# Depthwise convolution taps moved from diagonal matmuls on TensorE to scaled shifts on GpSimd, in an eight-core hybrid block

## Chip, cores and metric

One Trainium2 chip, all 8 cores. The batch has 4 sequences of 4,096 tokens; each core takes one half of one sequence (2,048 tokens), and for the state that the second half starts from it also reads the first half. No core talks to another. The metric is the device time of the slowest core in microseconds, the median over runs.

## What is computed

The block runs a gated linear recurrence (four heads of 128) beside a short gated convolution, merges the two with sigmoid gates, and ends with a SwiGLU feed-forward. The part that matters here is the convolution branch, 512 channels wide, with three causal taps for each channel:

```python
def short_conv_mixer(c_gate, b_gate, xb, conv_w):
    u = c_gate * xb                                          # inner gate C
    rhs = conv_w.astype(u.dtype)[:, None, :]                 # (K, 1, CONV_WIDTH) depthwise
    y = lax.conv_general_dilated(u, rhs, window_strides=(1,), padding=[(CONV_K - 1, 0)],
                                 dimension_numbers=('NWC', 'WIO', 'NWC'),
                                 feature_group_count=CONV_WIDTH)
    return b_gate * y                                        # outer gate B
```

`c_gate`, `xb` and `b_gate` are three slices of the input projection `h @ w_in`, where `h` is the normalised input. So for each channel c and token t, y(t) = w0 u(t-2) + w1 u(t-1) + w2 u(t), and the branch gives b(t) y(t).

## The kernel before

A core's 2,048 tokens are four blocks of T = 512. Activations lie transposed in SBUF, channels in the partitions: `hT0` to `hT3` hold the normalised input of the four blocks as 8 pieces of 128 channels by 512 tokens. Weights come as slabs of 1 MB (in memory) into a ring of 8 buffers, `ring0` to `ring7`, by DMAs that GpSimd issues (line 630); 0 holds the forget gate's slab, 1 the value slab, 2, 3 and 4 those of c, xb and b_gate, and 5, 6 and 7 first serve as buffers for arriving rows of x and later take the slabs of q, g and ga0.

`mm_fm` (line 737 before, 732 after) is the work horse: 8 matmuls of 128x512 into one PSUM bank. `conv_gen(b)` makes block b of the convolution. Its first loop runs over m = 0 to 3 (128 channels each): a c group of 8 matmuls, which ScalarE copies out of PSUM, then an xb group of 8, which VectorE multiplies by that copy into `u`, bf16, 514 columns wide so that two columns of the block before stand ahead. `u` is one buffer with one owner record: whoever reads any part of it waits for all four m, and the next block's first write waits for all of this block's readers. Its second loop, over m again, makes the outer gate. Before, that is 8 matmuls for b_gate and a ScalarE copy of them, then 3 matmuls with diagonal weights `diagw` on `u` shifted by 0, 1 and 2 columns (line 970), and a VectorE product of the two.

The engines' instruction order isn't the order of the program text. Generators are merged into one list of operations, and `Prog.schedule` then plays a list scheduler over it: each operation carries an assumed duration `dur`, each engine picks what it could start first, ties go by the place in the list, among the 48 nearest candidates. What comes out is a fixed order on each engine with semaphore waits. On the chip each engine then works through its own order strictly, so an instruction that waits holds up all behind it.

Around the four convolution blocks lie: norm and transpose work for the coming block (`norm_gen`, transposes at line 764), the recurrence's pass over the earlier half (`pf_gen`, `pv_gen`, `pt_gen`: lines 737, 746, 893, 910), and for block 3 the recurrence proper (`dense_gen` and `core_gen`; lines 1082, 1101, 1121 and 1123 are its small 128x128 matmuls, 1149 the sum over a head with `ones_f`).

Of the kernel before, what the change touches and what calls it, by code (L numbers as in the profile page):

```python
# [7 lines left out]
F32 = mybir.dt.float32  # L8
BF16 = mybir.dt.bfloat16
# [388 lines left out]
def build_nc():  # L398
# [11 lines left out]
    with ExitStack() as st:  # L410
        def sb(name, shape, dt):
            return st.enter_context(nc.sbuf_tensor(name, shape, dt))
# [6 lines left out]
        diagw = sb("diagw", [128, 12, 128], BF16)  # L419
# [277 lines left out]
        def late_consts():  # L697
            P.op("dve", lambda E: E.tensor_copy(out=cmask[:], in_=mskf), reads=[b_mskf], writes=[b_cmask])
            P.op("dve", lambda E: E.memset(ones_f[:], 1.0), writes=[b_ones])
            P.op("dve", lambda E: E.memset(smask[:], 1.0), writes=[b_smask])  # L700
            P.op("dve", lambda E: E.memset(smask[:].rearrange("p (c j) -> p c j", j=CH)[:, :, 0:1], 0.0),
                 reads=[b_smask], writes=[b_smask])
            for i in range(2):
                P.op("dve", lambda E, i=i: E.memset(AT[i][:], 0.0), writes=[b_AT[i]])
            for k in range(12):
                P.op("dve", lambda E, k=k: E.tensor_scalar(out=diagw[:, k, :], in0=ident[:], scalar1=cst[:, CW + k:CW + k + 1],
                                                           scalar2=0.0, op0=ALU.mult, op1=ALU.add),
                     reads=[b_ident, b_cst], writes=[b_diagw])
# [724 lines left out]
```

How the kernel before makes its waits and increments, by code:

```python
        def run(E, e):  # L300
            known = {}
            own = "P_" + e
            for i in self.order[e]:
                o = ops[i]
                need = {}
                for d in list(o.deps) + o.extra:
                    k, v = val[d]
                    if need.get(k, 0) < v:
                        need[k] = v
                for k, v in need.items():
                    if k == own and e == "pe":
                        continue
                    if known.get(k, 0) >= v:
                        continue
                    known[k] = v
                    E.wait_ge(self.sems[k], v)
                if o.chan is not None:
                    o.fn(E).then_inc(self.sems[o.chan], 16)
                else:
                    o.fn(E).then_inc(self.sems[own], 1)
            if e == "sp":
                for b in finals:
                    k, v = val[b.w]
                    if known.get(k, 0) < v:
                        known[k] = v
                        E.wait_ge(self.sems[k], v)
```

## Time and profile before

| | before |
|---|---|
| median of 3 runs | 1044.02 us (1042.1 to 1044.39) |
| profiled execution, its own time | 1040.56 us |
| span of its slowest core (core 5) | 1038.9 us (others 1034.0 to 1038.7) |
| TensorE matmul busy | 1005.8 us, 97% of the span |
| VectorE busy | 463.7 us, 45% |
| ScalarE busy | 414.9 us, 40% |
| GpSimd busy | 23.2 us, 2% |

The profiled execution's own time is 1.7 us more than the span. Busy times of one engine are sums over its instructions without overlap. Matmuls overlap in the pipeline, so a lone matmul's duration (379 ns for 128x512) is longer than the pitch at which a row of them proceeds; what a group costs is read from the rows of the chain, in which each piece follows the one before.

### The profile page before, as it was taken

To read this page: it belongs to the slowest core of one execution; us is meant where nothing else is said; L and a number is where in the kernel's file an instruction comes from. 1 tells how busy PE (TensorE), PEld (TensorE's weight loads), DVE (VectorE), ACT (ScalarE), POOL (GpSimd) and SP (SyncE) were. 2 spreads that over 40 slices of the span, in tenths; PEclk is the share of its full clock that TensorE was granted. 3 is DMA by queue.
4 is the path that set the end of the run, shared out by engine and by line. 5 is a ranking of instruction groups with operands and counts; after the bars stand their busy time and mean duration, and the time that the engine had idled before them with its cause. 6 is when DMAs were issued, how large, how long until landed. Compare 5 with 4: busy or idle time off the path is not lost.

```text
span 1038.9 us, 15069 instructions; the slowest of 8 cores (1034.0 to 1038.9 us)
## 1 busy us (share of the span) xinstructions
PE 1005.8 (97%) x5414; PEld 490.1 (47%) x5414; DVE 463.7 (45%) x651; ACT 414.9 (40%) x706; POOL 23.2 (2%) x49
## 2 busy tenths in 40 slices
PE   4799999999999999999999899999999999999997
PEld 4555545454545454444444444444444444444444
DVE  5777665576667576436564331212121121232223
ACT  3895743768677675233343321111111111111112
POOL 2000000000000000000000000000000000000000
PEclk9999999999999999999999999999999999999999
DMA  9993334033000262542337544020302216222211
GB/s 196 227 225 103 84 62 82 1 60 64 1 1 2 38 99 67 88 115 87 118 122 156 153 97 81 1 41 1 65 17 37 45 17 202 102 106 102 81 61 62
DMA packets 20233, 84.88 MB, mean 82 GB/s; under 512 B 2368, under 2 KB 2368, under 8 KB 16960
## 3 DMA queue, kind: packets, MB, share of 16 engines
q0 software_dynamic: 5904, 33.03, 19.3%
q1 hardware_dynamic: 14112, 50.62, 14.5%
q8 instruction: 45, 0.74, 0.3%
q14 instruction: 28, 0.23, 0.1%
q10 hardware_dynamic: 144, 0.26, 0.1%
HBM read 100.16 MB, written 16.78 MB: 113 GB/s over the span
## 4 chain that ended last, share of the span: by engine, by line
PE 93%; DMA 3%; ACT 2%; issue 1%; DVE 1%; SPq 0%; ACTq 0%; POOL 0%; DVEq 0%; POOLq 0%
PE pf L737 62%; PE pf L1284 15%; PE pf L746 9%; PE pf L764 2%; DMA ring<-x_prev 1%; PE pf L1149 1%; ACT arena L715 1%; DMA ring<-wall 1%; PE pf L970 1%; PE pf L795 1%; DVE arena L864 0%; PE pf L1121 0%; PE pf L830 0%; PE pf L1082 0%; PE pf L1101 0%
## 5 line engine op out<-in xcount | busy, mean ns | idle before, releaser
L737 PE MATMUL pf<-hT,ring 128*128 128x512 bf16 x2688 | 599.2, 379 | 2.3 <-ACT arena L715 1.9
L737 PEld LDWEIGHTS pf<-hT,ring 128*128 128x128 bf16 x2688 | 261.6, 98 | 314.4 <-issue 5.2
L1284 PE MATMUL pf<-ring,arena 128*128 128x512 bf16 (+1 forms) x726 | 152.2, 373 | 0.0
L715 ACT ACTIVATE arena<-pf 128x512 f32<-128x512 f32 (+3 forms) x164 | 99.0, 643 | 97.5 <-PE pf L737 86.1
L715 ACT ACTIVATE rtmp<-pf 128x512 f32<-128x512 f32 (+1 forms) x89 | 52.9, 595 | 186.8 <-PE pf L737 186.8
L1284 PEld LDWEIGHTS pf<-ring,arena 128*128 128x128 bf16 x726 | 71.0, 98 | 81.2
L719 DVE TENSOR_TENSOR arena<-rtmp,pf 128x512 bf16<-128x512 f32 (+1 forms) x69 | 46.9, 679 | 133.0 <-PE pf L737 128.2
L746 PE MATMUL pf<-ring,arena 128*128 128x512 bf16 x384 | 91.1, 384 | 3.7 <-DMA ring<-wall 3.4
L737 PE MATMUL pf<-arena,ring 128*128 128x512 bf16 x320 | 79.8, 379 | 0.9 <-ACT arena L715 0.9
L715 ACT ACTIVATE rtmp<-hT 128x1024 bf16<-128x1024 f32 (+2 forms) x18 | 17.3, 963 | 123.3 <-DVE hT L719 123.3
L719 DVE TENSOR_TENSOR arena<-arena 128x512 bf16<-128x512 f32 (+2 forms) x62 | 55.6, 897 | 23.1 <-ACT arena L715 20.8
L746 PEld LDWEIGHTS pf<-ring,arena 128*128 128x128 bf16 x384 | 37.5, 99 | 47.7 <-issue 6.1
L719 DVE TENSOR_TENSOR hT<-pf,hT 128x512 f32<-128x512 f32 (+1 forms) x33 | 22.3, 675 | 75.2 <-PE pf L1284 75.2
L715 ACT ACT_TABLE_LOAD x36 | 46.2, 1283 | 5.9 <-PE pf L1149 4.1
L727 DVE SCALAR_TENSOR_TENSOR arena<-arena,pf 128x512 f32<-128x512 f32 x44 | 30.1, 686 | 39.8 <-PE pf L737 33.6
L737 PEld LDWEIGHTS pf<-arena,ring 128*128 128x128 bf16 x320 | 30.1, 98 | 33.0 <-issue 1.5
L715 ACT ACTIVATE rtmp<-arena 128x1024 bf16<-128x1024 f32 (+1 forms) x24 | 25.3, 1053 | 45.9 <-DVE arena L727 45.9
L719 DVE TENSOR_TENSOR arena<-Wt,pf 128x512 bf16<-128x512 f32 x22 | 15.1, 688 | 60.0 <-PE pf L737 58.2
L719 DVE TENSOR_TENSOR hT<-pf,cst_sb 128x1024 bf16<-128x1024 bf16 x32 | 38.1, 1217 | 7.5 <-PE pf L764 7.5
L719 DVE TENSOR_TENSOR arena<-U,pf 128x512 bf16<-128x512 f32 x22 | 15.1, 687 | 58.1 <-PE pf L737 58.1
L630 POOL DMA_DIRECT2D ring<-wall x41 | 22.0, 538 | 830.0 <-PE pf L737 554.4
L715 ACT ACTIVATE arena<-ring 128x1024 bf16<-128x1024 f32 x32 | 33.8, 1056 | 15.2 <-PE pf L764 9.2
(96 smaller groups left out, 664.2 us busy)
## 6 DMA issues: line engine op xcount, KB each, us to landing
ring<-wall POOLq DMA_DIRECT2D x25, 1024.0 KB, 11.1
ring<-x_prev SPq DMA_DIRECT2D x16, 512.0 KB, 8.8
ring<-x_main SPq DMA_DIRECT2D x16, 512.0 KB, 4.7
arena<-x_main SPq DMA_DIRECT2D x16, 512.0 KB, 4.5
x1spill<-arena SPq DMA_DIRECT2D x16, 512.0 KB, 2.9
hT<-x1spill SPq DMA_DIRECT2D x16, 512.0 KB, 3.2
out<-hT SPq DMA_DIRECT2D x15, 512.0 KB, 2.6
ring<-wall POOLq DMA_DIRECT2D x6, 512.0 KB, 6.4
```

Source lines behind the costliest of these rows:

```text
L630: P.dma("pool", lambda E, s=s, idx=idx, a=a, z=z: E.dma_start(out=ring[s][:, a:z], in_=w_d[idx][:, a:z]), reads=need(gates[q]) if q < len( ...
L715: P.op("act", lambda E: E.activation(out=rs(out), in_=rs(in_), func=func, **kw), reads=reads, writes=writes, dur=dur, aset=ASET[func] if f ...
L719: P.op("dve", lambda E: E.tensor_tensor(out=rs(out), in0=rs(a), in1=rs(b), op=op), reads=reads, writes=writes, dur=0.17 + width(out, a, b) ...
L727: P.op("dve", lambda E: E.scalar_tensor_tensor(out=rs(out), in0=rs(a), scalar=s, in1=rs(b), op0=op0, op1=op1), reads=reads, writes=writes, ...
L737: last = E.matmul(pb(bk)[:, 0:ncol], lhsT=sl[:, o_:o_ + 128], rhs=rhs[:, c, :], start=(c == 0), stop=(c == kc - 1))
L746: last = E.matmul(pb(bk), lhsT=lhs(c), rhs=rhs_list[c], start=(c == 0), stop=(c == n - 1))
L764: last = E.transpose(out=tbv.res()[:, c * 128:(c + 1) * 128], in_=xs[:, c * 128:(c + 1) * 128], identity=ident[:])
L795: last = E.matmul(pb(bk)[:, c0:c0 + nc_], lhsT=sl[:, o_:o_ + 128], rhs=rhs[:, c, c0:c0 + nc_], start=(c == 0), stop=(c == 7), skip_group_c ...
L970: last = E.matmul(pb(by), lhsT=diagw[:, k * 4 + m, :], rhs=u[:, m, k:k + T], start=(k == 0), stop=(k == 2))
L1149: P.op("pe", lambda E, bk=bk, c=c: E.matmul(pb(bk), lhsT=ones_f[:], rhs=sqs[c][0], start=True, stop=True), reads=[b_ones, sqs[c][1]], writ ...
L1284: last = E.matmul(pb(bk)[:, 0:w], lhsT=act_v(c)[:, n * 128:(n + 1) * 128], rhs=rl[c], start=(c == 0), stop=(c == 21))
```

## The change

The diagonal weights and their 48 matmuls go, with the 12 VectorE instructions that made them, and so do the 16 ScalarE copies of b_gate. In their place GpSimd computes, for each block and each m, three scaled shifts of `u` (`pts`, one input, 128x512, bf16 in and float32 out) and two sums of these (`ptt`, two float32 inputs), into a scratch tile `a`. Then come the 8 matmuls for b_gate. They list `a` among what they read, so TensorE waits there for the whole GpSimd chain of this m, although the matmuls themselves don't touch it. VectorE then multiplies `a` by the PSUM bank.

Blocks 0 to 2 have two pairs of scratch tiles (`rtmp`, four tiles), block 3 has one pair (in `arena`). The c copies go to a new buffer `cvs` of two tiles.

```diff
-        def conv_gen(b, singles):
+        def pts(out, a, sc, reads, writes):
+            P.op("pool", lambda E: E.tensor_scalar(out=out, in0=a, scalar1=sc, scalar2=0.0, op0=ALU.mult, op1=ALU.add),
+                 reads=reads, writes=writes, dur=0.7)
+
+        def ptt(out, a, b, reads, writes):
+            P.op("pool", lambda E: E.tensor_tensor(out=out, in0=a, in1=b, op=ALU.add), reads=reads, writes=writes, dur=1.3)
...
+        def conv_gen(b, singles, tmps):
...
             for m in range(4):
+                (a, b_a), (q, b_q) = tmps[0], tmps[1]
+                if len(tmps) > 2:
+                    (a, b_a), (q, b_q) = tmps[2 * (m % 2)], tmps[2 * (m % 2) + 1]
+                pts(a, u[:, m, 0:T], cst[:, CW + m:CW + m + 1], [b_u, b_cst], [b_a])
+                pts(q, u[:, m, 1:T + 1], cst[:, CW + 4 + m:CW + 5 + m], [b_u, b_cst], [b_q])
+                ptt(a, a, q, [b_a, b_q], [b_a])
+                pts(q, u[:, m, 2:T + 2], cst[:, CW + 8 + m:CW + 9 + m], [b_u, b_cst], [b_q])
+                ptt(a, a, q, [b_a, b_q], [b_a])
                 bb = F_()
-                mm_fm(bb, sg, b_sg, m, 8, 0, hT, b_h)
-                i = cyc("p1s", singles)
-                actf(single(i), bank(bb), AF.Copy, [bb.buf], [b_T[i]])
+                mm_fm(bb, sg, b_sg, m, 8, 0, hT, list(b_h) + [b_a])
+                tt(yb_[b][0][:, m, :], a, bank(bb), ALU.mult, [b_a, bb.buf], [yb_[b][1]])
                 yield 8 * MMC
-                by = F_()
-
-                def fn(E, m=m, by=by):
-                    last = None
-                    for k in range(3):
-                        last = E.matmul(pb(by), lhsT=diagw[:, k * 4 + m, :], rhs=u[:, m, k:k + T], start=(k == 0), stop=(k == 2))
-                    return last
-                P.op("pe", fn, reads=[b_diagw, b_u], writes=[by.buf], dur=3 * MMC)
-                tt(yb_[b][0][:, m, :], single(i), bank(by), ALU.mult, [b_T[i], by.buf], [yb_[b][1]])
-                yield 3 * MMC
```

**TensorE, block 0.** The first fence is TensorE's order before, from the last xb group (`ring3`) of block 0 through its four b_gate groups (`ring4`):

```order
L737 MATMUL pf<-hT0,ring3 128x512 x8
L764 MATMUL pf<-ident,arena 128x128 x8
L737 MATMUL pf<-hT0,ring4 128x512 x8
L970 MATMUL pf<-arena,diagw 128x512 x3
L737 MATMUL pf<-hT0,ring4 128x512 x8
L764 MATMUL pf<-ident,arena 128x128 x8
L970 MATMUL pf<-arena,diagw 128x512 x3
L737 MATMUL pf<-hT0,ring4 128x512 x8
L970 MATMUL pf<-arena,diagw 128x512 x3
L737 MATMUL pf<-hT0,ring4 128x512 x8
L970 MATMUL pf<-arena,diagw 128x512 x3
```

The second is the same place after the change, from that same xb group to b_gate group 1:

```order
L732 MATMUL pf<-hT0,ring3 128x512 x8
L759 MATMUL pf<-ident,arena 128x128 x24
L888 MATMUL pf<-ident,arena 128x128 x8
L741 MATMUL pf<-ring1,arena 128x512 x8
L759 MATMUL pf<-ident,arena 128x128 x8
L741 MATMUL pf<-ring1,arena 128x512 x8
L905 MATMUL pf<-arena 128x128 x16
L759 MATMUL pf<-ident,arena 128x128 x8
L732 MATMUL pf<-hT0,ring4 128x512 x8
L741 MATMUL pf<-ring1,arena 128x512 x8
L732 MATMUL pf<-hT0,ring4 128x512 x8
```

It goes on with 8 transposes and 8 value matmuls, group 2, a c and an xb group of block 1, and group 3. The `ring4` groups, which used to follow the xb group at once, are now pulled apart, and other work stands in the gaps. What follows the last of them is held up with it.

**VectorE, block 2.** The next fence is VectorE's order after the change, from the last product into `u` of block 2 (`arena<-cvs,pf`) to the outer-gate products of m = 0 (first `arena<-rtmp,pf` behind the scan), 1, 2 and 3:

```order
L714 TENSOR_TENSOR arena<-cvs,pf 128x512
L714 TENSOR_TENSOR hT3<-pf,cst_sb 128x8x128 x2
L718 TENSOR_SCALAR arena<-arena,sv 128x512 x2
L815 SCALAR_TENSOR_TENSOR arena<-smask,arena 128x1024
L714 TENSOR_TENSOR arena<-rtmp,pf 128x512
L714 TENSOR_TENSOR arena<-arena 128x1024
L714 TENSOR_TENSOR arena<-rtmp,pf 128x512
L718 TENSOR_SCALAR arena<-arena,sv 128x512 x2
L714 TENSOR_TENSOR arena<-arena 128x1024
L958 COPY arena<-arena 128x4x2
L714 TENSOR_TENSOR arena<-rtmp,pf 128x512 x2
```

While GpSimd works on block 2's taps, VectorE has four scalings, a scan (printed as SCALAR_TENSOR_TENSOR with `smask`) and two products of two SBUF tensors of 1,024 columns to do. Counted in the same way, block 0 has six scalings of 1,024 columns (`arena<-ring,stat`) in that stretch, and block 1 four. In block 3 the same stretch holds four scalings of 512 columns, two scans, four products or sums of two SBUF tensors of 1,024 columns and five of 512.

**TensorE, block 3.** The last fence is TensorE's order after the change, from two of the `ones_f` sums to the third b_gate group of block 3; dense work of the recurrence's block 1 (`hT1` with `ring0`, `ring1`, `ring5`, `ring6`) stands between the groups:

```order
L1156 MATMUL pf<-arena,ones_f 128x512 x2
L732 MATMUL pf<-hT1,ring0 128x512 x8
L732 MATMUL pf<-hT3,ring4 128x512 x8
L1156 MATMUL pf<-arena,ones_f 128x512
L732 MATMUL pf<-hT1,ring0 128x512 x24
L732 MATMUL pf<-hT3,ring4 128x512 x8
L741 MATMUL pf<-ring1,hT1 128x512 x32
L732 MATMUL pf<-hT3,ring4 128x512 x8
```

Here the next m's chain can only start when the product of the m before has freed the one scratch tile, so the groups stand further apart; before, all four groups of this block stood ahead of the `ones_f` sums.

## Rows read from the trace of the kernel before

**Rows 1.** The page: busy time and instructions; the span in 40 slices, busy tenths.

```profile
PE 1005.8 (97%) x5414; PEld 490.1 (47%) x5414; DVE 463.7 (45%) x651; ACT 414.9 (40%) x706; POOL 23.2 (2%) x49
PE   4799999999999999999999899999999999999997
```

**Rows 2.** Busy time by stretch: length, busy (instructions), clock, DMA share, GB/s.

```profile
0.00:84.00 84.00, 62.72 (x589) 42.12 (x590) 57.02 (x88) 60.76 (x118) 7.13 (x19) 0.98 0.86 201
84.00:240.00 156.00, 153.50 (x901) 77.10 (x899) 94.90 (x128) 88.12 (x153) 3.69 (x7) 1.00 0.33 71
```

**Rows 3.** The chain that ended last, 100 to 240 us: start, length, what.

```profile
99.97 3.02 PE pf L737 x14
...
105.82 1.73 PE pf L737 x8
...
112.74 0.65 PE pf L970 x3
113.39 0.46 PE pf L764 x8
...
120.29 0.89 PE pf L910 x16
...
220.76 0.67 PE pf L1082 x12
...
235.24 3.43 PE pf L1149 x8
```

**Rows 4.** Instructions by shape: busy, mean ns of one, idle before them.

```profile
L970 PE MATMUL pf<-arena,diagw 128*128 128x512 bf16 x48 | 13.0, 379 | 0.0
L706 DVE TENSOR_SCALAR diagw<-ident,cst_sb 128x128 bf16<-128x128 bf16 x12 | 3.1, 262 | 1.0
L715 ACT ACTIVATE rtmp<-pf 128x512 f32<-128x512 f32 x88 | 52.8, 600 | 186.8 <-PE pf L737 186.8
```

**Rows 5.** GpSimd in order of time, 0.5 to 4 us: start, length.

```profile
0.60 0.10 POOL L399 MEMSET const-uint8-127<- 128x1 uint8 x1
...
3.04 0.22 POOL L678 MEMSET Wt<- 128x128 f32 x1
3.40 0.29 POOL L679 TENSOR_SCALAR_AFFINE_SELECT Wt<-Wt 128x128 f32<-128x128 f32 x1
```

**Rows 6.** VectorE in order of time, 102 to 104 us: start, length, wait ahead.

```profile
103.10 0.69 DVE L719 TENSOR_TENSOR arena<-rtmp,pf 128x512 bf16<-128x512 f32 x1 [2.10 <-PE pf L737]
```

**Rows 7.** GpSimd and VectorE in order of time, 6.2 to 7 us.

```profile
6.42 0.55 POOL L630 DMA_DIRECT2D ring<-wall  x1 [2.73 <-DMA ring<-x_prev]
6.62 0.35 DVE L706 TENSOR_SCALAR diagw<-ident,cst_sb 128x128 bf16<-128x128 bf16 x1
```

**Rows 8.** VectorE instructions by shape, as in rows 4.

```profile
L723 DVE TENSOR_SCALAR arena<-ring,stat 128x1024 bf16<-128x1024 f32 x32 | 23.6, 749 | 10.2 <-ACT stat L715 10.2
L723 DVE TENSOR_SCALAR arena<-arena,sv 128x512 f32<-128x512 f32 x32 | 16.4, 541 | 26.6 <-ACT arena L715 26.6
L820 DVE TENSOR_TENSOR_SCAN arena<-smask,arena 128x1024 f32<-128x1024 bf16 x8 | 18.3, 2286 | 0.6 <-ACT rtmp L715 0.5
L719 DVE TENSOR_TENSOR arena<-arena 128x1024 bf16<-128x1024 f32 x16 | 19.5, 1222 | 5.9 <-ACT arena L715 5.8
L719 DVE TENSOR_TENSOR Wt<-U,Gd 128x512 f32<-128x512 f32 x16 | 11.0, 686 | 0.9 <-DVE U L719 0.9
```

**Rows 9.** GpSimd in order of time, 84 to 260 us.

```profile
139.24 0.53 POOL L630 DMA_DIRECT2D ring<-wall  x1 [78.86 <-DVE arena L723]
...
167.80 0.53 POOL L630 DMA_DIRECT2D ring<-wall  x1 [13.67 <-ACT arena L715]
```

**Rows 10.** The longest of those transfers: microseconds from issue to landing, 100 to 240 us.

```profile
DMA to landing us min/median/max: 7.6/9.7/14.1
```

**Rows 11.** TensorE's waits, 0 to 300 us: microseconds in total, times, longest.

```profile
PE pf L764 <- DVE arena L723: 15.1, 5, 11.1
PE pf L737 <- ACT arena L715: 2.9, 3, 1.9
```

More of the change, by code:

```diff
@@ L418, in build_nc @@
         smask = sb("smask", [128, 2 * T], BF16)
-        diagw = sb("diagw", [128, 12, 128], BF16)
+        cvs = sb("cvs", [128, 2, T], F32)
         U = sb("U", [128, 4, 128], F32)
@@ L473, in bufs @@
             return [Buf(f"{pre}{i}") for i in range(n)]
-        b_cst, b_ident, b_ones, b_cmask, b_smask, b_diagw, b_U, b_W, b_sv, b_e1, b_G, b_e2l, b_zcol, b_hcol = (
-            Buf(n) for n in ["cst", "ident", "ones", "cmask", "smask", "diagw", "U", "W", "sv", "e1", "G", "e2l", "zcol", "hcol"])
+        b_cst, b_ident, b_ones, b_cmask, b_smask, b_U, b_W, b_sv, b_e1, b_G, b_e2l, b_zcol, b_hcol = (
+            Buf(n) for n in ["cst", "ident", "ones", "cmask", "smask", "U", "W", "sv", "e1", "G", "e2l", "zcol", "hcol"])
         b_Sb, b_AT, b_stat = bufs("Sb", 2), bufs("AT", 2), bufs("stat", 8)
@@ L704, in late_consts @@
                 P.op("dve", lambda E, i=i: E.memset(AT[i][:], 0.0), writes=[b_AT[i]])
[L705 to L708, printed above, removed]
         ASET = {AF.Exp: 1, AF.Ln: 1, AF.Silu: 2, AF.Tanh: 2}
@@ L919, in build_nc @@
         P1S = [10, 11, 12, 13]
+        P1T = [(single(i), b_T[i]) for i in P1S]
         def halo_gen():
@@ L940, in halo_gen @@
                ALU.mult, [bx.buf, b_T[i]], [b_u])
-        def conv_gen(b, singles):
+        def pts(out, a, sc, reads, writes):
[3 more added lines that the diff above has]
+            P.op("pool", lambda E: E.tensor_tensor(out=out, in0=a, in1=b, op=ALU.add), reads=reads, writes=writes, dur=1.3)
+        b_cvs = bufs("cvs", 2)
+        CVS = [(cvs[:, i, :], b_cvs[i]) for i in range(2)]
+        cv3 = []
+        for i in range(2):
+            v, bb = area(f"cv3_{i}", O_MG + 2 * 4096 + 2048 * i, 2048, F32)
+            cv3.append((v, bb))
+        def conv_gen(b, singles, tmps):
             sc, b_sc = slab("c")
@@ L951, in conv_gen @@
                 mm_fm(bc, sc, b_sc, m, 8, 0, hT, b_h)
-                i = cyc("p1s", singles)
-                actf(single(i), bank(bc), AF.Copy, [bc.buf], [b_T[i]])
+                cs_, b_cs = cyc("p1s" + str(b), singles)
+                actf(cs_, bank(bc), AF.Copy, [bc.buf], [b_cs])
                 yield 8 * MMC
@@ L956, in conv_gen @@
                 mm_fm(bx, sx, b_sx, m, 8, 0, hT, b_h)
-                tt(u[:, m, 2:T + 2], single(i), bank(bx), ALU.mult, [b_T[i], bx.buf], [b_u])
+                tt(u[:, m, 2:T + 2], cs_, bank(bx), ALU.mult, [b_cs, bx.buf], [b_u])
                 yield 8 * MMC
             for m in range(4):
+                (a, b_a), (q, b_q) = tmps[0], tmps[1]
[6 more added lines that the diff above has]
+                ptt(a, a, q, [b_a, b_q], [b_a])
                 bb = F_()
-                mm_fm(bb, sg, b_sg, m, 8, 0, hT, b_h)
-                i = cyc("p1s", singles)
-                actf(single(i), bank(bb), AF.Copy, [bb.buf], [b_T[i]])
+                mm_fm(bb, sg, b_sg, m, 8, 0, hT, list(b_h) + [b_a])
+                tt(yb_[b][0][:, m, :], a, bank(bb), ALU.mult, [b_a, bb.buf], [yb_[b][1]])
                 yield 8 * MMC
-                by = F_()
-                def fn(E, m=m, by=by):
-                    last = None
-                    for k in range(3):
-                        last = E.matmul(pb(by), lhsT=diagw[:, k * 4 + m, :], rhs=u[:, m, k:k + T], start=(k == 0), stop=(k == 2))
-                    return last
-                P.op("pe", fn, reads=[b_diagw, b_u], writes=[by.buf], dur=3 * MMC)
-                tt(yb_[b][0][:, m, :], single(i), bank(by), ALU.mult, [b_T[i], by.buf], [yb_[b][1]])
-                yield 3 * MMC
         P2_POOL = [2, 3, 4, 0, 1]
@@ L1340, in build_nc @@
         merge((seq(pf_gen(2), pt_gen(1), pv_gen(2)), 16.2), (norm_gen(hTs[0], mn(0)), 2.5))
-        merge((seq(halo_gen(), conv_gen(0, P1S)), 26.0), (norm_gen(hpre[1], hm(1)), 2.5))
+        merge((seq(halo_gen(), conv_gen(0, CVS, P1T)), 26.0), (norm_gen(hpre[1], hm(1)), 2.5))
         merge((seq(pf_gen(3), pt_gen(2), pv_gen(3)), 16.2), (norm_gen(hTs[1], mn(1)), 2.5))
-        merge((conv_gen(1, P1S), 23.4), (norm_gen(hTs[2], mn(2)), 2.5))
-        merge((conv_gen(2, P1S), 23.4), (norm_gen(hTs[3], mn(3)), 2.5), (pt_gen(3), 2.5))
+        merge((conv_gen(1, CVS, P1T), 23.4), (norm_gen(hTs[2], mn(2)), 2.5))
+        merge((conv_gen(2, CVS, P1T), 23.4), (norm_gen(hTs[3], mn(3)), 2.5), (pt_gen(3), 2.5))
         free.extend([5, 6, 7])
@@ L1349, in build_nc @@
                 drain(dense_gen(b))
-                merge((core_gen(0), 4.8), (conv_gen(3, [8, 9]), 23.4))
+                merge((core_gen(0), 4.8), (conv_gen(3, CVS, cv3), 23.4))
                 release("c", "xb", "bg")
```

## The prediction

> **What bounds the kernel now.** I read the busy line of the page first. TensorE is busy for 97% of the span and its digits are 9 nearly throughout, GpSimd for 2% [rows 1]. So a microsecond taken from TensorE's row of work is a microsecond of the time, as long as nothing makes TensorE wait. The table by stretch then tells where that holds. Up to 84 us TensorE is busy for 62.7 of 84 us with the DMA engines 86% full; the convolutions lie in 84 to 240 us, where it idles 156.0 - 153.5 = 2.5 us in all and GpSimd computes nothing, only issues weights [rows 2]. TensorE's own list of waits shows what such idle time is: short waits on ScalarE or VectorE, none on the convolution [rows 11]. The sum below is therefore made in 84 to 240 us, as a balance between matmuls taken out and new waits.
>
> **What comes out.** In the chain each trio of diagonal matmuls is a piece of 0.65 us, directly ahead of or behind the next group [rows 3]. There are 48 matmuls [rows 4], so 16 trios: 16 x 0.65 = **10.4 us off TensorE's path**. The 16 ScalarE copies (0.60 us each) and the 12 instructions that built the weights (3.1 us, early in the run, where the DMA engines are 86% full) lie on engines that wait for others [rows 2, 4]; I count both as nothing. If ScalarE were short of time in 84 to 240 us the copies would give something, but it is busy 88 of 156 us there [rows 2]. The outer product remains one VectorE instruction per m, only with operands from other places.
>
> **What comes in.** 80 GpSimd instructions, 20 a block. The trace has none of their kind. Next to them are a fill of 128x128 (0.22 us), a one-input select of 128x128 (0.29) and a fill of one column (0.10) [rows 5]. Stretched to 512 columns, the fill gives 0.10 + 4 x 0.12 = 0.58, the select 0.10 + 4 x 0.19 = 0.86. A scaled shift reads one input and does less than a select, so I put it between the two, at 0.72, with both ends as bounds. A sum reads two inputs: at least the select's 0.86, at most two passes, 1.72; I take 1.3, the middle. Between the fill and the select that waits for it lie 0.14 us beyond the fill's duration (3.04 + 0.22 to 3.40) [rows 5]; 14 of a block's 20 instructions wait so, 3.5 of the 5 of an m. An m then takes 3 x 0.72 + 2 x 1.3 + 3.5 x 0.14 = 5.25 us, a block 21.0 (bounds 3.95 and 6.5 an m, 15.8 and 26.1 a block).
>
> The Trainium skill (GPSIMD Engine Reference, section 3.1) times a two-input add of 2,048 columns at 4.5 us, a quarter of which is 1.12 us. By that figure, an estimate, a block would take 19.6 us in place of 21.0. No row here shows such an instruction.
>
> **How long TensorE can do without them.** Its four b_gate groups wait for the four chains, and TensorE takes its list in order, so every wait there is lost. I add up what stands ahead of the last group of each block after the block's last xb group, with the pieces of [rows 3]: 8 matmuls of 512 columns 1.73, 8 transposes 0.45, 16 small ones 0.89, a small one 0.056, an `ones_f` sum 0.86 (a quarter of 3.43).
> - Block 0: up to the first group (second fence) 5 x 0.45 + 0.45 + 2 x 1.73 + 0.89 = 7.05, then 7 x 1.73 + 0.45 more, so the last stands at 19.6.
> - Block 1: by the same count 20.9. Block 2: 22.1.
> - The chain begins when the last product into `u` is done, 0.8 us behind the xb group's end (103.10 + 0.69 = 103.79 against 99.97 + 3.02 = 102.99) [rows 3, 6], plus 0.1. So it ends at 0.9 + 21.0 = 21.9: **late by 2.3 and 1.0 us, and 0 in block 2**.
> - Block 3: the first group stands at 5.65, the chain ends at 0.9 + 5.25, 0.5 late. Each later m starts only when the product before is done: 0.8 + 0.1 + 2 x 0.72 + 2 x 1.3 + 0.4 = 5.3 us after a group, against 6.0, 6.9 and 7.1 us of other work. No wait, with 3.7 us in hand.
>
> That is 3.8 us of new waits if GpSimd has its memory to itself.
>
> **Whether it has.** Here one row speaks. While GpSimd issued a weight DMA (6.42 to 6.97 us) a VectorE scaling that began at 6.62 took 0.35 in place of 0.26 us, and ended at 6.97, with the DMA's issue [rows 4, 7]. So the two can hold each other up. After the change GpSimd reads SBUF nearly without a break for a block, and VectorE has scalings, scans and two-input products there. If each stops GpSimd for its length less the 0.14 us of pause that GpSimd has anyway [rows 5, 8]:
> - Block 0: 6 x (0.75 - 0.14) = 3.7. Block 1: 4 x 0.61 = 2.4.
> - Block 2: 4 x 0.40 + 2.15 + 2 x 1.08 = 5.9.
> - Block 3: 5 x 0.69 + 4 x 0.54 + 2 x 2.29 + 4 x 1.22 = 15.1 us of them, and GpSimd computes in 5.25 + 3 x 4.4 = 18.5 of some 33 us: 8.4, less the 3.7 in hand, 4.7.
>
> In blocks 0 to 2 GpSimd computes for some 0.85 of the stretch, and I count that share of 12.0: 10.2. The bounds are 0, if only a DMA's issue collides, and 16.7 with every operation counted in full. One collision of 0.09 us is thin evidence; I take the upper part, 14.9 - 1 (block 2 first uses up 0.2, block 1 nothing) = 14, because the row's end fits a wait until the other is done and not a slower pace.
>
> The Trainium skill (SBUF — State Buffer, section on who interferes with whom) says as much: a GpSimd operation and a VectorE one in a two-port mode, or with two SBUF inputs, exclude each other for the whole instruction. The 0.35 us in rows 7 agrees. That page speaks against this change. By the page all of the 16.7 us would count, without it none.
>
> **The sum.** -10.4 + 3.8 + 14 = +7.4. Of the 2.5 us for which TensorE already waits in this stretch [rows 2], some is absorbed, since VectorE and ScalarE catch up while TensorE stands: I take 1. **+6.4 us**. This execution's 1040.6 would become 1047.0, its span of 1038.9 1045.3. The median of the runs lies 3.4 us over this execution, and becomes **1050.5 us**.
>
> What stands behind the waiting group: on TensorE, value and transpose work of the recurrence's pass; on VectorE, the two-column copy of `u` for the next block (it waits for GpSimd's last read) and behind it the scalings and scans of `pf_gen(3)`, which TensorE needs a few microseconds later. That is why I take the waits as lost and not as moved.
>
> **The weight loads in GpSimd's queue.** Three loads now queue among the chains; before they went out between 139 and 168 us, with nothing else on GpSimd, and landed within 7.6 to 14.1 us, 9.7 in the middle [rows 9, 10]. The tightest is q's: it stands before the last two operations of block 1's chains, so it goes out 0.9 + 21.0 - 2.0 + 2.4 = 22.3 us behind that block's last xb group, and lands at 32.0, at the latest at 36.4. Its first use stands at 20.9 + 7 x 1.73 + 2 x 0.45 = 33.9, plus the waits of block 1. I count it as nothing; the slowest landing would cost up to 2 us.
>
> **The rivals.**
> - *The chains hide* (31%). GpSimd and VectorE hardly disturb each other, or the shifts cost 0.58 and the sums 0.9 to 1.1. For it: at the lower bounds a block takes 15.8, far below 19.6. Against it: the row on the collision. Time: -10.4 + 3.8 - 1 = -7.6 with the middle costs, 1036.4; -10.4 at the lower bounds, 1033.6.
> - *The costs meet the gain* (13%): middle costs with half of the collisions, -10.4 + 3.8 + 7 - 1 = -0.6, 1043.4.
> - *The forecast* (44%): the chains late in each block, 1046 to 1056.
> - *GpSimd at its upper bounds* (12%): 26.1 us a block is late by 7.4, 6.1 and 4.9, and block 3 by 2.4: 20.8 in place of 3.8. With the collisions that is 17 more than forecast, 1067.5. This one is decided by the sum's duration: from about 1.5 us on.
>
> The change can't do nothing: the matmuls are gone and 80 instructions stand in.
>
> **The numbers.** The point is the forecast's. Slower by over 0.2% (2.1 us, about what a measurement of this kernel can tell from no change) is the forecast and the upper rival, 0.56; within it 0.13; faster 0.31. The range cuts off a tenth at either end: 1035 from the first rival, 1064 between the last two. The forecast's own range is 1046 to 1056.
>
> **What the changed profile would show.** No line 970, and TensorE's busy time less by about 10. GpSimd busy for some 75 to 100 us more, all in 84 to 250 us; shifts near 0.7, sums near 1.3, longer where VectorE works beside them. TensorE waiting for GpSimd at line 732, mostly at the last groups of a block, 15 us or more in all. If the shortest sums take under 1.1 us and TensorE waits for GpSimd under 8 us, the forecast is wrong and the kernel is faster. If a sum takes over 1.5 us with VectorE idle, the upper rival holds. If VectorE's scalings of 0.75 us are not longer in block 0, the collision step is wrong.

## Result: 0.24% slower, +2.5 us where +6.4 was forecast

| | before | after |
|---|---|---|
| median of 12 runs each, taken on the same chips | 1043.07 us | 1045.66 us |
| ratio of the runs | 1 | 1.0024 [1.0014, 1.0033], so +2.5 us (1.5 to 3.4) |
| span of the profiled execution's slowest core | 1038.9 us | 1043.9 us (core 7; the others 1038.8 to 1043.4) |

The spans of two single executions also hold some scatter at the start. To compare kernels with less noise I read two instructions in each trace: the last start of the small halo matmuls, just ahead of the first block's convolution, and the last start of the state matmuls behind block 3's. The groups of those lines, with min/median/max of a duration in ns and first and last start, of before (core 5):

```profile
L931 PE MATMUL pf<-hcol,ring x64: 163/163/167, 65.1 to 81.9; 128*128 128x2 bf16 x64
L1101 PE MATMUL pf<-arena x64: 219/219/219, 218.4 to 399.9; 128*128 128x128 bf16 x64
```

and of after (core 7):

```profile
L927 PE MATMUL pf<-hcol,ring x64: 163/163/167, 66.4 to 83.2; 128*128 128x2 bf16 x64
L1108 PE MATMUL pf<-arena x64: 219/219/219, 218.7 to 404.5; 128*128 128x128 bf16 x64
```

The stretch between them is 399.9 - 81.9 = 318.0 us before and 404.5 - 83.2 = 321.3 after; as a mean over the eight cores 317.86 and 320.85, **+3.0 us**. I call it the conv stretch. Ahead of it after is 0.7 us later, behind it 1.1 us slower up to the last layer and 0.4 faster there. So the change acts within this stretch, and its +3.0 lies inside the interval of the runs.

Of the page of after, busy time and the busy tenths of TensorE and GpSimd:

```profile
PE 1002.1 (96%) x5366; PEld 487.4 (47%) x5366; DVE 470.8 (45%) x639; ACT 406.4 (39%) x690; POOL 112.1 (11%) x129
PE   4799899999999999999999899999999999999997
POOL 2000727737000000000000000000000000000000
```

Against [rows 1] TensorE has 48 matmuls less, GpSimd 88.9 us more, in the fifth to tenth slice. TensorE's digits hardly show a loss. The table by stretch does (length, busy with instructions for TensorE, weight loads, VectorE, ScalarE, GpSimd, then granted clock, DMA share, GB/s):

```profile
84.00:240.00 156.00, 146.41 (x854) 72.46 (x853) 102.81 (x129) 84.44 (x146) 74.78 (x75) 0.99 0.33 67
```

In 84 to 240 us TensorE now idles 156.0 - 146.4 = 9.6 us, against 2.5 in [rows 2]. Who it waited for in 84 to 290 us (total, times, longest):

```profile
PE pf L732 <- POOL arena L943: 3.6, 3, 1.5
PE pf L732 <- POOL rtmp L943: 2.9, 3, 1.5
PE pf L888 <- DVE hT L714: 1.7, 1, 1.7
PE pf L741 <- DVE hT L714: 1.1, 2, 0.5
PE pf L759 <- DVE arena L718: 1.0, 1, 1.0
```

6.5 us for GpSimd's sums (7.4 on core 1), 3.8 for VectorE in these lines. The places, from TensorE's timeline (start, length, line, tiles, in brackets the wait ahead):

```profile
104.15 1.50 PE L759 MATMUL pf<-ident,arena 128*128 128x128 bf16 x24
109.25 0.61 PE L759 MATMUL pf<-ident,arena 128*128 128x128 bf16 x8 [0.98 <-DVE arena L718]
122.49 8.79 PE L732 MATMUL pf<-hT,ring 128*128 128x512 bf16 x40 [1.48 <-POOL rtmp L943]
147.55 1.13 PE L759 MATMUL pf<-ident,arena 128*128 128x128 bf16 x16
150.35 1.20 PE L888 MATMUL pf<-ident,arena 128*128 128x128 bf16 x16 [1.66 <-DVE hT L714]
152.07 3.43 PE L741 MATMUL pf<-ring,hT 128*128 128x512 bf16 x8 [0.53 <-DVE hT L714]
172.82 5.34 PE L732 MATMUL pf<-hT,ring 128*128 128x512 bf16 x24
178.00 1.06 PE L759 MATMUL pf<-ident,arena 128*128 128x128 bf16 x16
202.53 10.52 PE L732 MATMUL pf<-hT,ring 128*128 128x512 bf16 x48 [0.31 <-POOL rtmp L943]
```

GpSimd's instructions by shape (busy us, mean ns of one | idle before):

```profile
L943 POOL TENSOR_TENSOR rtmp<-rtmp 128x512 f32<-128x512 f32 x24 | 31.9, 1338 | 1.5 <-POOL rtmp L939 0.5
L939 POOL TENSOR_SCALAR rtmp<-arena,cst_sb 128x512 f32<-128x512 bf16 x36 | 30.9, 868 | 57.4 <-DVE arena L714 56.2 <-POOL rtmp L943 0.9 <-PE pf L905 0.2
L939 POOL TENSOR_SCALAR arena<-arena,cst_sb 128x512 f32<-128x512 bf16 x12 | 13.7, 1141 | 6.8 <-DVE arena L714 3.6 <-PE pf L1156 1.9 <-POOL arena L943 1.2
L943 POOL TENSOR_TENSOR arena<-arena 128x512 f32<-128x512 f32 x8 | 12.6, 1570 | 1.5 <-POOL arena L939 0.5
```

and min/median/max of those of blocks 0 to 2:

```profile
L939 POOL TENSOR_SCALAR rtmp<-arena,cst_sb x36: 682/692/2506, 105.3 to 200.2; 128x512 f32<-128x512 bf16 x36
L943 POOL TENSOR_TENSOR rtmp<-rtmp x24: 1253/1266/1722, 107.3 to 201.0; 128x512 f32<-128x512 f32 x24
```

A shift alone takes 0.69 us and a sum 1.26 (0.72 and 1.3 assumed). I read what lies above that, up to the longest shift of 2.51 us, as collisions with VectorE. Two of them in block 3, from the timelines of GpSimd and VectorE:

```profile
244.67 2.29 DVE L815 TENSOR_TENSOR_SCAN arena<-smask,arena 128x1024 f32<-128x1024 bf16 x1
244.81 2.65 POOL L939 TENSOR_SCALAR arena<-arena,cst_sb 128x512 f32<-128x512 bf16 x1 [2.19 <-DVE arena L714]
...
247.60 2.20 POOL L943 TENSOR_TENSOR arena<-arena 128x512 f32<-128x512 f32 x1
248.59 1.50 DVE L718 TENSOR_SCALAR arena<-arena,sv 128x512 f32<-128x512 f32 x1
```

A shift that starts 0.14 us behind a scan takes 2.65 us: the scan's remaining 2.15 (to 246.96) and 0.50 of its own. A scaling that takes 0.54 us alone [rows 8] takes 1.50 behind a sum, and ends 0.29 us after it. So each waits nearly until the other's end, in both directions.

### The profile page after: what moved, and what is told of

The parts are those of the page before. It is cut to its first block, busy times and chain, and to the rows that moved or that the text cites. A ratio compares the mean times of both kernels' runs of the same rounds, so it can differ in the third digit from the quotient of the medians.

```text
span 1043.9 us, 15057 instructions; the slowest of 8 cores (1038.8 to 1043.9 us)
## 1 busy us (share of the span) xinstructions
PE 1002.1 (96%) x5366; PEld 487.4 (47%) x5366; DVE 470.8 (45%) x639; ACT 406.4 (39%) x690; POOL 112.1 (11%) x129
## 4 chain that ended last, share of the span: by engine, by line
PE 88%; POOL 3%; issue 3%; DMA 3%; DVE 2%; ACT 1%; SPq 0%; POOLq 0%; DVEq 0%; ACTq 0%
PE pf L732 60%; PE pf L1291 15%; PE pf L741 8%; PE pf L759 2%; DMA ring<-x_prev 1%; DMA ring<-wall 1%; PE pf L1156 1%; POOL arena L943 1%; POOL arena L939 1%; PE pf L790 1%; POOL rtmp L943 1%; DVE arena L714 1%; POOL rtmp L939 1%; ACT arena L710 0%; DVE arena L859 0%
## 5 line engine op out<-in xcount | busy, mean ns | idle before, releaser
L710 ACT ACTIVATE arena<-pf 128x512 f32<-128x512 f32 (+3 forms) x156 | 94.2, 643 | 100.7 <-PE pf L732 85.9
L714 DVE TENSOR_TENSOR arena<-rtmp,pf 128x512 bf16<-128x512 f32 (+1 forms) x57 | 38.6, 678 | 127.9 <-PE pf L732 125.8
L710 ACT ACTIVATE rtmp<-pf 128x512 f32<-128x512 f32 (+1 forms) x65 | 38.5, 593 | 145.1 <-PE pf L732 145.1
```

Source lines behind the costliest of these rows:

```text
L710: P.op("act", lambda E: E.activation(out=rs(out), in_=rs(in_), func=func, **kw), reads=reads, writes=writes, dur=dur, aset=ASET[func] if f ...
L714: P.op("dve", lambda E: E.tensor_tensor(out=rs(out), in0=rs(a), in1=rs(b), op=op), reads=reads, writes=writes, dur=0.17 + width(out, a, b) ...
```

## Experiments

Four theories were set against each other. **A**: the chains are late for TensorE, as forecast; only what exceeds the gaps in TensorE's order costs. **B**: VectorE is held up by GpSimd's accesses, whoever waits for the chains. **C**: the changed order and dependences cost, not GpSimd's time. **D**: the loss is in proportion to GpSimd's busy time. "Stretch" is the conv stretch, mean of eight cores, from one execution of each kernel.

Two kinds of experiment stand in the table. In `x1_tiny`, `x5_half` and `x9_448` TensorE, VectorE and ScalarE go through this stretch in exactly the order of after, and in `x2_dummy` in that of before. All the others change a dependence, an assumed duration or an engine, so the planner made a new order for every engine: what they show is the edit and its new order together.

| kernel | ratio to before, 95% | stretch, us | against before |
|---|---|---|---|
| before | 1 | 317.86 | 0 |
| after | 1.0024 [1.0014, 1.0033] | 320.85 | +3.0 |
| `x1_tiny`: GpSimd on 8 columns | 0.992 [0.9907, 0.9932] | 310.10 | -7.8 |
| `x5_half`: on 256 columns | 0.9931 [0.9918, 0.9944] | 310.12 | -7.7 |
| `x9_448`: on 448 columns | 0.999 [0.9978, 1.0002] | 317.07 | -0.8 |
| `x2_dummy`: before, plus 80 GpSimd operations | 1.0016 [1.0006, 1.0026] | 319.32 | +1.5 |
| `x3_nodep`: b_gate groups don't wait | 1.008 [1.0068, 1.0092] | 327.18 | +9.3 |
| `x4_dur`: planner told longer durations | 1.0051 [1.0034, 1.0067] | 323.19 | +5.3 |
| `x6_own`: `u` owned per m | 0.9955 [0.9941, 0.9969] | 312.22 | -5.6 |
| `x10_ownnd`: x6 and x3 | 0.9929 [0.9904, 0.9954] | 311.41 | -6.4 |
| `x7_act`: shifts on ScalarE, and x3 | 1.0026 [1.0016, 1.0035] | 320.94 | +3.1 |
| `x8_ownact`: x6 and x7 | 0.9911 [0.9897, 0.9925] | 308.49 | -9.4 |

### GpSimd's time taken out, every order kept (x1_tiny)

```diff
-  E.tensor_scalar(out=out, in0=a, ...)
+  E.tensor_scalar(out=out[:, 0:8], in0=a[:, 0:8], ...)
-  E.tensor_tensor(out=out, in0=a, in1=b, op=ALU.add)
+  E.tensor_tensor(out=out[:, 0:8], in0=a[:, 0:8], in1=b[:, 0:8], op=ALU.add)
```

It leaves out 504 of the 512 columns of the taps; one fill of `rtmp` stands ahead of block 0.

> The change with every engine's order kept, but each of the 80 GpSimd operations works on 8 columns in place of 512 (504 of 512 columns of the taps are left out; the scratch tiles are filled once by GpSimd at 50 to 85 us). Theory A (TensorE pays the late chains and nothing else): without them the full price of the diagonal matmuls comes back, 10.4 us less than the kernel before plus up to 2 us for the new order, ratio to before 0.990 to 0.992. Theory C (the new order itself costs most of the 13 us that were lost): ratio 0.998 to 1.002.

Measured -7.8 us. C is out as the main cause: with all instructions, dependences and orders in place but short chains, the change is a gain. Of the 10.4 us of matmuls 2.6 are missing, a little more than A's "up to 2". That is what the new order costs by itself, and most of it can be seen. TensorE waits 4.2 us in the stretch, none of it for GpSimd, where before has 2.5. The largest place lies in block 1 (compare the same rows of after above):

```profile
147.50 1.13 PE L759 MATMUL pf<-ident,arena 128*128 128x128 bf16 x16
150.30 1.20 PE L888 MATMUL pf<-ident,arena 128*128 128x128 bf16 x16 [1.66 <-DVE hT L714]
152.03 1.89 PE L741 MATMUL pf<-ring,hT 128*128 128x512 bf16 x8 [0.53 <-DVE hT L714]
```

So the waits of 1.66 and 0.53 us for VectorE in after aren't made by GpSimd's chains. GpSimd's chains at full width cost the rest, 320.85 - 310.10 = **10.75 us**, where the forecast had 3.8 + 14 = 17.8.

### The same GpSimd work beside the old kernel, waited for by nobody (x2_dummy)

```diff
+  dum = sb("dum", [128, T], BF16)
...
             for m in range(4):
+                dts(0); dts(1); dtt(); dts(2); dtt()   # GpSimd: read hT[b], write dum
                 bb = F_()
```

The diagonal matmuls and all orders of the other engines are as before. `dts` and `dtt` wait for the products into `u` as the real chains do.

> The kernel before, every other engine's order unchanged, with 80 GpSimd operations of the same kinds and widths added, whose results nobody reads and which wait only for each product into u. Theory A: nobody waits for them, so only what VectorE loses by collisions could reach TensorE, and most of that is hidden: 0 to 2 us, ratio 1.000 to 1.002; GpSimd's shortest shift 0.69 and sum 1.26 us, longer beside VectorE's scans. Theory B (the price is VectorE held up by GpSimd, whoever waits): 5 to 13 us, ratio 1.005 to 1.012.

```profile
L970 POOL TENSOR_TENSOR dum<-dum,hT 128x512 bf16<-128x512 bf16 x32 | 38.1, 1190 | 4.9 <-POOL dum L965 0.5
L965 POOL TENSOR_SCALAR dum<-hT,cst_sb 128x512 bf16<-128x512 bf16 x48 | 35.3, 736 | 63.3 <-DVE arena L720 56.0 <-POOL dum L970 4.6 <-POOL dum L965 2.7
```

73 us of GpSimd work cost +1.5 us (0.6 to 2.7 by the runs), which is about a seventh of the 10.75 us (6 to 25%). So B is not the main cause. The work collides less than the real one, though. VectorE's 290 instructions of the stretch take 7.2 us longer in all than in before, and in after 12.0 longer than in `x1_tiny`. GpSimd's take some 3.5 us more than alone (means of 1.19 and 0.74 us against 1.15 and 0.69), and in after 16.2 (worked out below). Scaled by VectorE's loss the price would be 2.4 us, an estimate.

### How long the chains may be (x5_half, x9_448)

The edit is x1's with 256 and with 448 columns; 256 and 64 columns of the taps are left out.

> The change with all orders kept and each GpSimd operation on 256 of its 512 columns (half of the taps left out). The stretch of the four convolutions took 310.1 us with 8 columns and 320.9 with 512. Theory A (a threshold: it costs only as far as the chain is longer than the gap that the order leaves): a block's chains shrink to about 12 us, below every gap, so the stretch takes 310 to 312 us and the ratio to before is 0.992 to 0.994. Theory D (cost in proportion to GpSimd's busy time, as collisions would be): 315 to 316 us, ratio 0.997 to 0.998.

> The change with all orders kept and each GpSimd operation on 448 of its 512 columns (an eighth of the taps left out). From the lone durations at 512 and 256 columns an m's chain gets 0.5 us shorter, a block's four 2 us, about what collisions with VectorE added to a block in blocks 0 to 2 of the change (22.1 against 20.5 us). Theory A: past the threshold each microsecond of chain costs one of TensorE, so 5 to 8 us of the 10.7 come back, stretch 313 to 316 us; and as much of the loss is then what the collisions add. Theory D (proportional): 1.3 us come back, 319.5 us.

At 256 columns a sum takes (mean)

```profile
L943 POOL TENSOR_TENSOR rtmp<-rtmp 128x256 f32<-128x256 f32 x24 | 18.0, 758 | 1.2
```

and the stretch is that of 8 columns, 310.12 against 310.10: GpSimd is busy for twice as long (50.3 us against 25.0 in 84 to 240 us) and nothing is lost. D is out. At 448 columns 7.0 us of the 10.75 are there, and at 512 the last 64 columns cost 3.8 of it, where D had 1.3. So there is a threshold, as A has it, but A had expected a stretch of 313 to 316 us at 448 columns. Part of that miss is TensorE's clock: on cores 0 to 3 the granted clock over 146 to 156 us was 0.83 and the stretch 317.6 to 318.3 us, on cores 4 to 7 it was 1.00 and the stretch 315.9 to 316.6. At full clock 448 columns so cost 5.8 to 6.5 us. VectorE's 290 instructions are longer than in `x1_tiny` by 3.9 us in all at 256 columns, by 12.5 at 448 and by 12.0 at 512: most of the collisions come with the same step as most of the loss. That they cause it is not shown.

### The wait moved off TensorE (x3_nodep)

```diff
-  mm_fm(bb, sg, b_sg, m, 8, 0, hT, list(b_h) + [b_a])
+  mm_fm(bb, sg, b_sg, m, 8, 0, hT, b_h)
```

Now only VectorE's product waits for the chain, and the planner, which sees b_gate matmuls that are free to run, orders all engines anew.

> The change with the scratch tile taken off the b_gate matmuls' list of reads; only VectorE's product still waits for the chain. Theory A: TensorE no longer stands for GpSimd, but the products come late and hold PSUM banks and VectorE's queue, so part of the 13 us comes back: ratio to before 0.992 to 0.999. Theory B: the disturbance stays, ratio 1.001 to 1.004, as with the change.

It lost another 6.3 us, which neither theory had. VectorE's list of waits, 84 to 290 us:

```profile
DVE arena L714 <- POOL rtmp L943: 17.9, 7, 5.7
DVE arena L714 <- POOL arena L943: 8.6, 4, 4.1
```

VectorE stands 26.5 us for GpSimd, with the evictions of transposed tiles behind it in its queue, for which TensorE in turn waits:

```profile
124.08 1.01 PE L888 MATMUL pf<-ident,arena 128*128 128x128 bf16 x8 [5.74 <-DVE arena L714]
125.22 3.57 PE L741 MATMUL pf<-ring,arena 128*128 128x512 bf16 x8
```

The row of 8 behind that stop takes 3.57 us in place of the 1.89 of the row in `x1_tiny` above, and the table by stretch has the granted clock below full there (third number from the right, 0.92, of 84 to 150 us):

```profile
84.00:150.00 66.00, 55.46 (x330) 27.76 (x334) 41.24 (x51) 31.94 (x66) 18.76 (x20) 0.92 0.25 81
```

All eight cores have that 0.92. By these rows the lower clock makes up some 2 us of the 6.3 (1.7 in the row of 8, 0.4 in the 8 transposes ahead of it), an estimate. So in after the dependence on `a`, which the matmuls don't need, keeps the wait out of VectorE's queue. How much of the 6.3 us is the wait moved and how much the new order was not separated.

### Truer durations for the planner (x4_dur)

```diff
-  reads=reads, writes=writes, dur=0.7)      # shift
+  reads=reads, writes=writes, dur=1.0)
-  reads=reads, writes=writes, dur=1.3)      # sum
+  reads=reads, writes=writes, dur=1.55)
```

> The change with 1.0 and 1.55 us in place of 0.7 and 1.3 as the durations that the scheduler assumes for GpSimd, about what shifts and sums took at the most crowded places; the instructions are the same, the gaps ahead of the b_gate groups get wider. Theory A: the waits for GpSimd shrink from 6.5 us to under 2 and the late starts with them: ratio to before 0.993 to 0.999. Theory B: unchanged, 1.001 to 1.004.

Worse by 2.3 us than the change; neither theory had that. The planner now spreads the groups further, but GpSimd, sent in the new order, waits for scratch tiles that VectorE frees later, and TensorE still waits for it:

```profile
119.48 1.66 POOL L939 TENSOR_SCALAR rtmp<-arena,cst_sb 128x512 f32<-128x512 bf16 x2 [1.81 <-DVE arena L714]
...
123.74 1.36 POOL L939 TENSOR_SCALAR rtmp<-arena,cst_sb 128x512 f32<-128x512 bf16 x2 [1.38 <-PE pf L732]
```

```profile
PE pf L732 <- POOL rtmp L943: 4.4, 2, 2.8
PE pf L732 <- POOL arena L943: 2.9, 2, 2.1
```

7.3 us for GpSimd, against 6.5. The longest of these waits, 2.8 us, is followed by a row of 8 matmuls that takes 3.35 us in place of 1.89. Over 150 to 176 us the granted clock is 0.93 on all eight cores. That alone is 1.5 of the 2.3 us, an estimate. Telling the planner these longer durations brought nothing back.

### The chain of m started when its own part of `u` is there (x6_own, x10_ownnd)

```diff
-  u_v, b_u = area("u", O_MG, 4112)
+  b_u = [reg(f"u{m}", "arena", O_MG + 1028 * m, 1028) for m in range(4)]
...
+                if b > 0:     # halo columns of this m alone, ahead of its product
+                    P.op("dve", lambda E, m=m: E.tensor_copy(out=u[:, m, 0:2], in_=u[:, m, T:T + 2]), reads=[b_u[m]], writes=[b_u[m]])
-  pts(..., [b_u, b_cst], ...)
+  pts(..., [b_u[m], b_cst], ...)
```

Same arithmetic, same instructions, except that the copy of two columns for all four m becomes four. GpSimd may start m = 0 while TensorE still works on c and xb of m = 1 to 3.

> The change with u tracked as four parts, one for each m, and its two-column copy for the next block made for each m: the same arithmetic, but the chain of m = 0 can start when its own product is done and not that of m = 3, some 10 us earlier. Theory A (late chains are the price): nearly all of the 10.7 us between 8 and 512 columns comes back, stretch 311 to 314 us, ratio to before 0.992 to 0.997. Theory D (collisions between GpSimd and VectorE are the price): there are as many of them, stretch 319 to 321 us, ratio 1.001 to 1.003.

> u tracked for each m, all arithmetic on GpSimd, and the b_gate matmuls without the scratch tile in their list. Where the chain starts late, taking that dependence away cost 6.3 us (stretch 327.2 against 320.9). Theory A: with the chains early it matters less, stretch 311 to 315 us against 312.2 with the dependence. If the dependence itself is harmful once the chains are early: 309 to 311.

-5.6 us: `x6_own` is 8.6 us faster than after, as A had it. TensorE's table shows that it idles 156.0 - 150.3 = 5.7 us in place of 9.6, at clock 1.00. GpSimd's instructions:

```profile
L944 POOL TENSOR_TENSOR rtmp<-rtmp 128x512 f32<-128x512 f32 x24 | 31.9, 1337 | 1.8
L940 POOL TENSOR_SCALAR rtmp<-arena,cst_sb 128x512 f32<-128x512 bf16 x36 | 26.4, 742 | 61.2 <-DVE arena L715 59.9 <-POOL rtmp L944 1.2
L944 POOL TENSOR_TENSOR arena<-arena 128x512 f32<-128x512 f32 x8 | 11.8, 1471 | 1.2
L940 POOL TENSOR_SCALAR arena<-arena,cst_sb 128x512 f32<-128x512 bf16 x12 | 10.8, 906 | 34.8 <-DVE arena L715 29.5 <-PE pf L1157 2.1 <-PE pf L1109 1.7
```

```profile
84.00:240.00 156.00, 150.33 (x873) 75.40 (x887) 110.11 (x143) 87.50 (x150) 79.00 (x83) 1.00 0.31 68
```

Three things changed at once here. The chains start earlier (block 0's at 93.3 us in place of 105.3, both on the slowest core). GpSimd loses half as much: its instructions exceed their lone durations by 8.0 us, by their counts and means, against 16.2 in after. And the planner's new order has fewer waits of another kind. On a core whose clock stayed at 1.00 in after (core 1) TensorE waits 7.4 us for GpSimd and 5.8 for other engines, 4.2 of which `x1_tiny` has too; in `x6_own` (core 0) it waits 4.4 and 1.1. So of 7.7 us of waits that are gone 3.0 were for GpSimd. The 8.6 us can't all be put down to earlier chains, and D's condition, as many collisions as before, wasn't met.

With early chains the dependence no longer matters much: x10 without it is another 0.8 us shorter, and by the runs the two are not told apart.

### Shorter chains (x7_act), and both (x8_ownact)

```diff
-  pts(a, u[:, m, 0:T], cst[:, CW + m:CW + m + 1], [b_u, b_cst], [b_a])
+  actf(a, u[:, m, 0:T], AF.Copy, [b_u, b_cst], [b_a], scale=cst[:, CW + m:CW + m + 1])
```

The same for the other two shifts, and x3's edit; the sums stay on GpSimd. x8 has x6's owners too.

> The three scaled shifts of each m on ScalarE, only the two sums on GpSimd, and the b_gate matmuls no longer list the scratch tile; u tracked as one buffer. ScalarE was busy 84 of 156 us in this stretch and gets 48 x 0.6 = 29 us more. Theory A: GpSimd's part of a block falls from 20.5 to 11 us, but the product still stands in VectorE's queue as in the run that took the dependence away (stretch 327 us): 313 to 322 us, ratio 0.994 to 1.004. If ScalarE becomes what is waited for: above 324 us.

> Both together: u tracked for each m, shifts on ScalarE, sums on GpSimd, no dependence of the matmuls on the scratch tile. Theory A: the chains are short and start early, stretch 308 to 312 us, ratio to before 0.990 to 0.995, the fastest so far. If the extra ScalarE work holds up the c copies, 313 to 318.

x7 is where the change is, +3.1 us, though its GpSimd is busy for half as long; beside x3, which has the same dependences, it is 6.2 us better. Both came within what A had expected. x8 is -9.4 us, 1.0 short of the 10.4 that the matmuls took, and faster than both kernels: 0.9911 of before. Its table has TensorE idle 2.15 us in the stretch, less than before the change:

```profile
84.00:240.00 156.00, 153.85 (x904) 77.28 (x902) 106.39 (x143) 115.81 (x196) 45.25 (x39) 1.00 0.36 75
```

## Why the prediction was right in sign and too high

**Where it stood.** Forecast +6.4 us, measured +2.5 (1.5 to 3.4). The 1045.7 us lie just below the forecast's own range of 1046 to 1056, and inside the wide one. By the bound of 0.2% the ratio says slower, though with an interval that reaches to both sides of it.

**What came out** (10.4 us): x8 shows 9.4 of it and x1 7.8, so the size is right. Its other side was counted at nothing: the new order of TensorE and VectorE. The sum even took 1 us off for waits that would be absorbed. In x1 the new order costs 2.6 us, of which 4.2 - 2.5 = 1.7 are TensorE's waits; the other 0.9 was not traced.

**What comes in.** Shift 0.69 us (0.72), sum 1.26 (1.3), a pause between dependent ones of 0.15 to 0.17 (0.14). These prices held. The chains of blocks 0 to 2 were shorter than 21.0 us all the same. With two pairs of scratch tiles the planner lets two m overlap, so that 4 to 7 pauses are left of the 14 a block that the prediction counts: what a block took, less what its instructions exceeded their lone durations, was 19.6, 20.0 and 18.7 us. Block 1's holds two weight loads that GpSimd issued in it, 0.6 us each; the prediction had no term for them.

**The gaps.** From the end of the last xb group to the start of the block's last b_gate group, by the same instruction of TensorE's order in each trace (after by core 2, at clock 1.00; block 3 is the sum of its four steps from group to group):

| us | prediction's count | `x1_tiny` | after | chains cost | forecast |
|---|---|---|---|---|---|
| block 0 | 19.6 | 20.8 | 23.5 | 2.7 | 5.4 |
| block 1 | 20.9 | 23.6 | 25.0 | 1.4 | 3.0 |
| block 2 | 22.1 | 22.1 | 24.5 | 2.5 | 4.8 |
| block 3 | 30.8 | 31.6 | 35.9 | 4.3 | 5.2 |

The chains cost 10.9 us by this table, as by the stretch (10.75). The forecast column adds the collisions to the lateness (2.3 + 3.7 x 0.85, 1.0 + 2.0, 4.8, 0.5 + 4.7) and gives 18.4; the prediction's own sum is 17.8, because it took 1 us off where its count takes off 0.2. Against the count after loses 15.5 us, but 4.7 of these are in x1 too.

Block 1 shows the difference best. Its chain starts 150.98 - 147.55 = 3.4 us behind the xb group in place of 0.9:

```profile
150.98 2.02 POOL L939 TENSOR_SCALAR rtmp<-arena,cst_sb 128x512 f32<-128x512 bf16 x3 [7.46 <-DVE arena L714]
```

VectorE is the reason, with work of its own: it has gone without a break since 143.98 us, and makes the last product into `u` only at 150.12:

```profile
147.27 0.66 DVE L714 TENSOR_TENSOR arena<-cvs,pf 128x512 bf16<-128x512 f32 x1
147.85 1.22 DVE L714 TENSOR_TENSOR arena<-arena 128x1024 bf16<-128x1024 f32 x1
148.98 1.22 DVE L714 TENSOR_TENSOR hT<-pf,cst_sb 128x1024 bf16<-128x1024 bf16 x1
150.12 0.68 DVE L714 TENSOR_TENSOR arena<-cvs,pf 128x512 bf16<-128x512 f32 x1
```

GpSimd has nothing to do with it: in x1, with 8 columns, the chain starts as late (3.4 us behind), and TensorE stands for VectorE at the same place. The two-column copy that the prediction names did wait for GpSimd, 4.4 us, but at the end of block 2 (200.96 us), and the product behind it then waited another 1.2 us for TensorE, so it held nothing up there.

TensorE's row of 8 at 152.07 us took 3.43 us on core 7, where x1 has 1.89. Only cores 5 and 7 have that (granted clock 0.83 over 146 to 156 us, 1.00 on the other six), and their stretches, 320.6 and 321.2 us, are no longer than the others' 320.3 to 321.0: in block 1 the others wait for GpSimd instead, 1.0 us in all.

**The step that failed** is the price of late chains, 3.8 + 14 = 17.8 us, where the runs show 10.75. Three things in it were off in blocks 0 to 2. The chains without collisions took 18.7 to 20.0 us and not 21.0. Collisions lengthened them by 2.1, 1.7 and 4.4 us and not by 3.1, 2.0 and 5.0. And TensorE had more time before it needed the last one, 20.8 and 23.6 us in blocks 0 and 1 and not 19.6 and 20.9, since it waits for VectorE in that stretch anyway. In all, by counts and means, GpSimd's instructions exceed their lone durations there by 24 x (1.338 - 1.26) + 36 x (0.868 - 0.69) = 8.3 us (forecast 10.2), and in block 3 by 12 x (1.141 - 0.69) + 8 x (1.570 - 1.26) = 7.9 (forecast 8.4).

The second error runs the other way: 1 us absorbed, where the new order costs 2.6. So 7.05 us too much and 3.6 too little leave the 3.4 between +6.4 and the stretch's +3.0. That the forecast came this near is in part luck. The mechanism, chains that come late for TensorE, is the one that x1 and x5 show; what share of the 10.75 us the collisions have stays open.

The forecast of "15 us or more" of TensorE waiting for GpSimd is wrong as such: it waits 6.5 us (7.4 on core 1).

The Trainium skill (SBUF — State Buffer, who interferes with whom) has a GpSimd instruction and a VectorE one in a two-port mode exclude each other for a whole instruction, and says that one with two SBUF inputs contends with GpSimd's reads too. The trace agrees, by the pairs at 244.67 and 247.60 us. How much of it reaches the end only a run can tell; the prediction went too far towards all.

**The forecast of the checks.** GpSimd +88.9 us (75 to 100 forecast). TensorE's busy time fell by 3.7 us, where about 10 was forecast; the rest was not traced. VectorE's scalings of 0.75 us are longer in block 0, up to 1.85 us:

```profile
L718 DVE TENSOR_SCALAR arena<-ring,stat x6: 737/776/1847, 107.3 to 121.9; 128x1024 bf16<-128x1024 f32 x6
```

**What stays open.** How much of the 10.75 us collisions cost inside the real chains: they can't be taken out without changing who works on what. x2 has 1.5 us for bf16 work that nobody waits for and that collides less. Why the loss between 8 and 256 columns is nil and at 448 already 7.0 is not resolved between collisions and plain length. How much of x6's gain is the earlier start and how much the planner's new order is open too; x6's owners with after's order would tell.

## What to carry to other kernels

Work put on an idle engine need not cost its busy time; it costs its lateness against the place in the waiting engine's order. With half of the columns the loss was gone, with an eighth less about a third of it. Price that lateness against a trace or a run in which the helper's work is nearly empty and all orders are kept: here that showed that 2.6 us of the loss were the new order and not the helper. Before a late helper is made faster, look at what holds its start: here one owner record for four parts of `u` kept it waiting for all of them, and splitting it, with the order that the planner then made, gave 8.6 us. A dependence that looks useless may decide which in-order queue does the waiting; taking it away, again with a new order, moved the wait from TensorE to VectorE and cost 6.3 us. And where a planner sets the orders, hardly any edit changes one thing alone.

## What the runs showed of the hardware

- Some instructions of GpSimd and VectorE exclude each other to the end of the other's: a shift of 0.69 us took 2.65 beside a scan of 2.29, a scaling of 0.54 us took 1.50 behind a sum. VectorE's products of a PSUM operand with `cst_sb` didn't get longer (1.20 to 1.22 us in before and after). 80 GpSimd instructions beside an unchanged kernel cost 1.5 us of 318.
- A GpSimd sum of two float32 operands of 512 columns takes 1.26 us, on 256 columns 0.72; of two bf16 operands of 512 columns 1.15. A scaled shift from bf16 takes 0.69 us. Between dependent ones stand 0.15 to 0.17 us.
- After a wait TensorE's granted clock can fall, and the wait then costs more than its own length (1.00 is the 2.4 GHz level, the other one is 1.2). After 5.7 us of waiting in x3 a row of 8 matmuls took 3.57 us in place of 1.89, with a granted clock of 0.92 over 84 to 150 us on all eight cores; after 2.8 us in x4 3.35. But it can also stay: after the same waits of 1.66 and 0.53 us the row took 3.4 us on two cores of after, and 1.89 on the other six and on all of x1.
